# Nine unread products on TensorE around the last expert's down stage, in a two-layer decoder step

## The reference, cut to what matters

```python
def moe_ffn(x, w_router, w1, w3, w2):
    probs = jax.nn.softmax((x @ w_router).astype(jnp.float32), axis=-1)
    top_p, top_i = lax.top_k(probs, TOP_K)
    top_p = top_p / jnp.sum(top_p, axis=-1, keepdims=True)
    gates = jnp.sum(jax.nn.one_hot(top_i, N_EXPERTS, dtype=jnp.float32) * top_p[..., None], axis=-2)
    y = jnp.zeros(x.shape, jnp.float32)
    for e in range(N_EXPERTS):
        y = y + gates[..., e:e + 1] * swiglu(x, w1[e], w3[e], w2[e]).astype(jnp.float32)
    return y.astype(x.dtype)
...
    y_prompt = rmsnorm(h_p, norm_final)[:, N_META:]
    y_sample = rmsnorm(h_s, norm_final)
```

## Time and profile before

| what | value |
|---|---|
| median of 3 runs | 901.18 us (900.46 to 905.54) |
| profiled execution, its own time | 898.49 us |
| its span, first to last instruction | 896.7 us |
| PE busy | 839.2 us (94% of the span) |
| DVE, ACT, POOL busy | 505.3, 450.2, 227.5 us |
| mean granted TensorE clock | 0.945 |

### The profile page before, as it was taken

One profiled execution on the slowest core, in us unless ns is written; L12 is line 12 of the kernel. 1 busy time (PEld: TensorE's weight loads), 2 busy tenths in 40 slices (PEclk: granted clock), 3 DMA queues, 4 the chain that ended last, 5 costly groups with the idle time before them and its releaser, 6 DMA issues.

```text
span 896.7 us, 12536 instructions
## 1 busy us (share of the span) xinstructions
PE 839.2 (94%) x5109; PEld 762.3 (85%) x5109; DVE 505.3 (56%) x777; ACT 450.2 (50%) x654; POOL 227.5 (25%) x77
## 2 busy tenths in 40 slices
PE   4899999999999999997999999989999999999985
PEld 3688789999999999897998878768888988888874
DVE  5998433222221111196453554667697787969864
ACT  3925635434434444625632233247585675766752
POOL 4000026677776775674310000000000000000000
PEclk9979799999999999999885899998999999999987
DMA  9409236535535534644363004376697967969601
GB/s 368 108 1 106 9 100 234 188 101 201 185 125 191 195 128 150 253 168 160 126 228 158 1 29 167 118 284 235 261 334 287 360 214 308 300 254 363 249 1 50
DMA packets 39755, 163.62 MB, mean 182 GB/s; under 512 B 12616, under 2 KB 13912, under 8 KB 32144
## 3 DMA queue, kind: packets, MB, share of 16 engines
q1 hardware_dynamic: 31184, 152.19, 47.2%
q10 hardware_dynamic: 5984, 1.54, 3.0%
q0 software_dynamic: 2528, 9.06, 2.9%
HBM read 156.56 MB, written 6.22 MB: 182 GB/s over the span
## 4 chain that ended last, share of the span: by engine, by line
PE 57%; issue 14%; POOL 12%; DVE 9%; ACT 6%; DMA 2%; POOLq 0%; DVEq 0%; ACTq 0%
POOL w_lo L538 11%; PE pair L2043 6%; PE pair L2049 6%; PE pair L2044 6%; PE pair L1659 5%; PE pair L1627 4%; PE pair L1629 4%; PE pair L1628 4%; PE pair L2073 3%; PE pair L2077 3%; PE pair L2074 3%; PE pair L2092 2%; ACT work L635 1%; PE pair L1692 1%; PE pair L2023 1%
## 5 line engine op out<-in xcount | busy, mean ns | idle before, releaser
L538 POOL TENSOR_TENSOR w_lo<-ring,w_hi 128x2048 fp32r<-128x2048 f32 x45 | 206.8, 4602 | 137.6 <-ACT w_hi L713 137.6
L997 DVE TENSOR_TENSOR m_lo<-ring,m_hi 128x1792 fp32r<-128x1792 f32 (+1 forms) x120 | 193.8, 1649 | 54.1 <-ACT m_hi L840 53.6
L840 ACT CAST m_hi<-ring 128x1792 fp32r<-128x1792 f32 (+1 forms) x120 | 165.8, 1394 | 86.2 <-PE pair L2049 47.2
L1627 PE MATMUL pair<-x_hi,w_hi 128*128 128x280 f32 x544 | 162.6, 299 | 3.5 <-DVE work L1265 2.9
L1628 PE MATMUL pair<-x_lo,w_hi 128*128 128x280 f32 x544 | 161.0, 296 | 0.0
L1629 PE MATMUL pair<-x_hi,w_lo 128*128 128x280 f32 x544 | 161.0, 296 | 0.0
L713 ACT CAST w_hi<-ring 128x2048 fp32r<-128x2048 f32 x45 | 85.8, 1907 | 79.9 <-PE pair L1629 79.9
L1627 PEld LDWEIGHTS pair<-x_hi,w_hi 128*128 128x128 f32 x544 | 104.9, 193 | 5.2 <-DVE work L1265 3.3
L1628 PEld LDWEIGHTS pair<-x_lo,w_hi 128*128 128x128 f32 x544 | 105.0, 193 | 0.1
L1629 PEld LDWEIGHTS pair<-x_hi,w_lo 128*128 128x128 f32 x544 | 104.8, 193 | 0.0
L2043 PE MATMUL pair<-m_hi,xg_hi 128*128 128x448 f32 x256 | 94.5, 369 | 0.9 <-ACT xg_lo L873 0.9
(11 more groups left out here) (363 smaller groups left out, 1397.8 us busy)
## 6 DMA issues: line engine op xcount, KB each, us to landing
ring<-in_main SPq DMA_DIRECT2D x58, 1024.0 KB, 4.9
ring<-in_up SPq DMA_DIRECT2D x64, 896.0 KB, 6.5
ring<-in_down SPq DMA_DIRECT2D x56, 512.0 KB, 5.4
work<-in_sgla POOLq DMA_DIRECT2D x8, 512.0 KB, 5.0
out_glas<-work POOLq DMA_DIRECT2D x8, 512.0 KB, 3.5
xT<-in_xT SPq DMA_DIRECT2D x1, 1120.0 KB, 5.4
out_yT<-xn ACTq DMA_DIRECT2D x4, 132.0 KB, 1.8
out_yT<-xn SPq DMA_DIRECT2D x4, 132.0 KB, 1.8
```

The costliest lines, as they stand in the source:

```text
L538: nc.gpsimd.tensor_tensor(w_lo[i % 3][:, :, :], ring[:, i % RAW, :].rearrange("p (t m) -> p t m", m=P), w_hi[i % 3][:, :, :].bitcast(F32), ...
L840: nc.scalar.copy(m_hi[n % NHI][:, 0:size], ringf[:, at_:at_ + size]).then_inc(hi_ready, 1)
L997: v.tensor_tensor(m_lo[:, at_:at_ + size], ringf[:, at_:at_ + size], m_hi[n % NHI][:, 0:size].bitcast(F32), ALU.subtract).then_inc(lo_read ...
L1627: mm(out, wh, hi, start=start, stop=False)
```

## The change

`keep_running` gets the bank as a second argument, with the old bank as its default. In the last expert (NE - 1, expert 7) it is called with 3 products behind the register read and in front of the transposes, after a new wait for x_ready that makes sure the bank banks[0] (half of pairs[3]) is no longer needed by the scatter of pair 2; with 2 products behind the transposes, in the same bank; and with 4 products behind the loop, in front of the last pair's scatter, in the bank pairs[1][:, 1]. Each product is two instructions on PE.

```diff
-            def keep_running(n):
+            def keep_running(n, bank=pairs[0][:, 0, :]):
                 for _ in range(n):
-                    mm(pairs[0][:, 0, 0:TM], ident, xn[:, DC - 1, M0:], start=True, stop=True)
+                    mm(bank[:, 0:TM], ident, xn[:, DC - 1, M0:], start=True, stop=True)
...
                         flag = pe.value_load(more[0:1, 0:1], min_val=0, max_val=1)
+                        pe.wait_ge(x_ready, DC * (2 + NPAIR))
+                        keep_running(3, banks[0])
                     transposes(e)
+                    if e == NE - 1:
+                        keep_running(2, banks[0])
                     if e:
                         pe.wait_ge(y_lo_ready, 2 * e)
                     down(e)
+            keep_running(4, pairs[1][:, 1, :])
             for m in range(DC):
                 scatter(NPAIR - 1, m)
             sum_squares(4)
```

## The result

| | before | after |
|---|---|---|
| median of 19 runs | 901.14 us (893.97 to 910.06) | 896.92 us (889.68 to 915.99) |
| ratio | 1 | 0.9943, 95% interval 0.9918 to 0.9969 |
| profiled execution | 898.49 us, span 896.7 us | 904.28 us, span 902.5 us |

By the ratio the changed kernel is faster by 0.57%, or 5.1 us of 901, with 2.8 to 7.4 us as the interval; the two medians differ by 4.2 us, or 0.47%. The ratios in this document leave out the executions that lie over 1.5% above the fastest of their kernel, here five of the nineteen of after (904.28 to 915.99 us), and so 5.1 us may be too much. The forecast was 897.6 us, range 895.8 to 900.5, a gain of 3.6.

A forecast was written before the change was run, and what follows sets the result against it. TensorE, busy in 94% of the span, was taken to end the kernel at half speed in two stretches. Winning 2.47 and 1.5 from 901.18 gives 897.2; a median gain of 3.6 was chosen: 897.6 us, range 895.8 to 900.5.

The forecast's parts named there:

- down stage: Last expert's down products up to the array coming free: 12.23 us would become 9.76 at full clock, gain 2.47 us.
- scatter: Last scatter's 32 products: 5.52 us would become 4.0 at full-clock spacing, gain 1.5 us.
- Expert 6 as a template: Expert 6's last four down units at full clock, 1.383 us each, used to price the last expert's down stage.
- nothing: Added products in the last expert's three waits: zero cost at full clock, with 1.2, 0.47 and 0.37 us of cover left.
- cover behind the transposes: Second wait: two products end at 864.67, first down product starts at 865.14, so 0.47 us is left.
- register read: TensorE's queue ahead of the first three products: between 0 and 1.4 us, taken as 0.
- Whether the grant holds: Last expert's waits: filling leaves 1.2, 0.5 and 0.4 us idle, and the clock stays at 1.00; forecast chance 0.70.
- Rival 2: Unread products sharing one stationary tile don't hold the grant, which falls before the transposes: 901.9 to 903.3 us; chance 0.06.
- Rival 1: Grant still falls in the first wait despite three products; only the scatter's 1.5 is won: 900.2 us; chance 0.16.
- Rival 3: The median run of before has little of either low stretch, gaining under 2.5: about 899.5 us; chance 0.08.
- size for a median run: Whole kernel: gain between 2.5 (second low stretch absent) and 4.8 (transposes slow too), taken as 3.6 us.
- table load of ScalarE: Behind the last square, for the root: moves with the scatter, ends near 885.9, ahead of the sum of squares at 887.3.

The follow-up runs named there:

- e1: Changed kernel without the four unread products in front of the last scatter; ratio to before 0.9976 (0.9934 to 1.0018).
- e2: Changed kernel with only the four products in front of the last scatter, the other two calls taken out; ratio to before 0.9965 (0.9931 to 1.0).
- e4: Changed kernel with 12, 8 and 16 transposes of 128x128 instead of the 3, 2 and 4 products; ratio to before 0.9939 (0.9907 to 0.997).
- e8: Changed kernel plus six products in front of expert 0's transposes and two behind them; ratio to before 0.9872 (0.9825 to 0.992).
- e9: The changed kernel itself run again, in the same rounds as the repeat with expert 0 filled; ratio to before 0.9949 (0.9901 to 0.9998).
- e10: Changed kernel with expert 0's waits filled too, run again beside the change; ratio to before 0.9944 (0.9897 to 0.9992).
- e5: Changed kernel with only the three products in front of the transposes; ratio to before 0.9923 (0.9874 to 0.9971).
- e7: Changed kernel with six products instead of two behind the transposes; ratio to before 0.991 (0.9864 to 0.9956).
- e3: Changed kernel with all nine products 8 columns wide instead of 264, same places and waits; ratio to before 1.0039 (1.0 to 1.0079).
- e6: Changed kernel with only the two products behind the transposes; ratio to before 0.9984 (0.9941 to 1.0027).

## Why the prediction was right

The term for the **down stage** was 2.47 us. Measured from its first product to the scatter, it went from 19.88 - 5.50 = 14.38 to 17.42 - 5.50 = 11.92, 2.46 us less. The term for the **scatter** was 1.5 us; it went from 5.52 to 4.01, 1.51 us. Their sum of 4.0 is the tail's 3.97. e1 and e2 show each by itself. Expert 6 as a template at full clock was what made the first term exact.

The costs that I had put at **nothing** were nothing, and the covers were as worked out: transposes 3.40 and down products 5.50 us behind the up line in both kernels. The cover behind the transposes was put at 0.47 and was 0.39. The **register read**, bounded by 0 and 1.4 us, takes nothing that can be seen: the first unread product starts at 870.21, 0.82 us behind the start of the last four up products, where the array comes free (0.81 in the prediction).

**Whether the grant holds** was the step with the least behind it. It held in all five profiles with the full filling (after, e4, e8, e9, e10), and in e5 and e7. Rival 2, that such products don't hold it, is refuted by the same profiles. Rival 1, a fall in the first wait in spite of the three products, came in none of these seven and not in e1; the rule of the Trainium skill on transposes, which would have given the same, is refuted for this kernel by e4. Rival 3, that an execution of before mostly has little of either low stretch, has the four profiles with no wide products in the first wait (before, e2, e3, e6) against it: each has the first stretch, of 6.8, 6.8, 6.8 and 3.4 us. Rival 1's price of 900.2 was also too high: I let the low stretch keep its length while two products ran in it, and e6, the nearest thing to it, shows a return 3.4 us after the fall. Its scatter starts 1.18 us sooner behind the up line than in before (18.70 against 19.88), where rival 1 had it 0.5 us later; with the scatter's 1.5 us that rival would have been worth 2.7 us, some 898.5 (an estimate from that one profile).

The **size for a median run**, 3.6 us, was a choice between 2.5 and 4.8, on the ground that a wait of 2 us doesn't always bring the low level. That ground held (the low level came in three of five), and by those shares the mean gain would be 2.5 + 0.6 x 1.5 = 3.4 us, if the first stretch always cost what it did here; five profiles are few for such a share. The measured ratio says 5.1 us with 2.8 to 7.4, so it can't tell 3.4 from 4.0, and that the median came out within 0.7 us of the forecast is partly luck. By the ratio the change is over 0.5% faster, an outcome that the prediction gave 0.22, against 0.74 for less; no profile shows more than 3.97 us, 0.44%, so the rest of the 5.1 lies in the sample. What the prediction missed is the spread of the runs: I took the 2.7 us between profile and median for an unexplained offset, while the two profiles of before and after differ by some 10 us in the attention stage alone.

Two of its sums are off, without effect. The table load of ScalarE was placed at 885.9 us and the sum of squares's end at 887.3 with the scatter's 1.5 us alone; with both gains they are 883.4 and 884.8, in the same order, and in after the load ends at 893.21, ahead of the root's start at 894.58. And the low end of the range is 901.18 - 4.8 - 0.7 = 895.7, not 895.8.

## What to carry to other kernels

Where TensorE waits a few microseconds for a chain on other engines, read the granted clock behind the wait: the wait itself may be fixed, but the products behind it can be running at half pace (0.43 us apart for 0.23 in the down stage here), and unread work in the wait can buy them back, 2.46 and 1.51 us in this kernel. Price the filling by the stream from start to start, put in only what ends ahead of the release at full clock, and remember that the time of filling beyond the cover was paid nearly in full (e7). Compare such kernels by a stretch of the trace between two fixed instructions, since the totals of single executions move by more than the effect.

## What the runs showed of the hardware that I had not expected

Transposes of 128x128 fp32 hold the granted clock like products: 27 of them, with a wait of 1.11 us between and 0.25 us behind, at 1.00 throughout (e4). Nine products of 8 columns in the same places, with 1.85 us left idle in front of the transposes, don't (e3). The same wait of 2.00 us in front of the scatter is followed by the low level in some executions (before, e1) and not in others (e5, e6), and the low stretch behind the first wait lasted 3.4 us in one kernel (e6) and 6.8 in the others. And a low stretch of the attention stage that began near 474.5 us ended near 502 us in one execution (before) and not before 528.5 in another (after), worth some 10 us, more than anything the change does.
